# Ring slots, half slots of rounded weights and six feature buffers at other addresses in a three-block transformer kernel

## The reference

```
x = first_block(x, ...)    # h @ w_in; latent attention + a two-way RWKV scan; two branch products; w_out
x = second_block(x, ...)   # x @ w_in_2; conv, pooling and Fourier branches; w_out_2; gated FFN 2048 -> 5632 -> 2048
x = third_block(x, ...)    # c @ w_ada; h @ w_in_3; two attentions; w_out_3; gated FFN 2048 -> 5504 -> 2048
...
def conv_ffn(h, w_up, conv_w, conv_b, w_down):
    u = h @ w_up
    ...
    return (jax.nn.silu(gate) * val) @ w_down
```

## Time and profile before

| | |
|---|---|
| time, median of 3 runs | 3411.87 us (3408.52 to 3414.73) |
| the profiled execution, first to last instruction (span) | 3388.4 us |
| the median's distance from that span | 23.5 us |
| PE busy | 3255.3 us, 96% |
| PEld busy | 3103.4 us, 92% |
| DVE busy | 2275.4 us, 67% |
| ACT busy | 1517.0 us, 45% |
| mean HBM traffic | 196 GB/s |

### The profile page before, as it was taken

How to read it: one execution, slowest core, us unless ns; L and a number is a source line. 1 busy time by engine, 2 the same in 40 slices (tenths; PEclk the granted TensorE clock), 3 DMA queues, 4 the chain that set the end, 5 groups by cost and what they waited for, 6 DMA issues and landing times.

```text
span 3388.4 us, 71888 instructions
## 1 busy us (share of the span) xinstructions
PE 3255.3 (96%) x30322; PEld 3103.4 (92%) x30322; DVE 2275.4 (67%) x2978; ACT 1517.0 (45%) x1835; POOL 74.3 (2%) x154
## 2 busy tenths in 40 slices
PE   8999899999998999999999999999989999999998
PEld 8998888888898769999999999989879899999998
DVE  8776856565687977777655544565656777777545
ACT  5442454443244035544444343453454555545443
POOL 0000100000000000000000000000000000000000
PEclk9999999999999999999999999999999999999999
DMA  8758723232786544677655555534424455555554
GB/s 322 261 204 329 273 86 107 86 108 92 279 346 238 187 161 175 252 290 283 240 190 194 193 195 198 187 127 165 159 100 163 162 191 192 186 187 193 190 197 152
DMA packets 94146, 664.19 MB, mean 196 GB/s; under 512 B 10353, under 2 KB 10993, under 8 KB 15346
## 3 DMA queue, kind: packets, MB, share of 16 engines
q1 hardware_dynamic: 74736, 540.05, 44.4%
q0 software_dynamic: 14400, 104.86, 8.0%
q10 hardware_dynamic: 4802, 16.12, 1.2%
HBM read 654.70 MB, written 6.29 MB: 195 GB/s over the span
## 4 chain that ended last, share of the span: by engine, by line
PE 86%; DVE 9%; ACT 2%; issue 1%; DMA 1%; ACTq 0%; SPq 0%; DVEq 0%
PE ps L463 22%; PE ps L462 22%; PE ps L464 21%; PE ps L434 4%; PE ps L657 4%; PE ps L641 2%; PE ps L493 2%; PE ps L642 2%; PE ps L643 2%; DVE ring_parts L1837 2%; DVE work L1860 1%; DVE work L2113 1%; PE ps L506 1%; DVE ring_parts L1845 1%; PE ps L650 1%
## 5 line engine op out<-in xcount | busy, mean ns | idle before, releaser
L1837 DVE TENSOR_TENSOR ring_parts<-ring,ring_hi 128x1024 fp32r<-128x1024 f32 x866 | 1042.1, 1223 | 701.2 <-ACT ring_hi L1158 687.3
L1158 ACT ACTIVATE ring_hi<-ring 128x1024 fp32r<-128x1024 f32 x866 | 909.4, 1059 | 1141.6 <-PE ps L464 1094.9
L463 PE MATMUL ps<-h_lo,ring_hi 128*128 128x256 f32 x2624 | 729.2, 278 | 0.0
L462 PE MATMUL ps<-h_hi,ring_hi 128*128 128x256 f32 x2112 | 593.1, 281 | 15.8 <-DVE h_lo L1867 8.5
L464 PE MATMUL ps<-h_hi,ring_parts 128*128 128x256 f32 x2112 | 585.1, 277 | 0.0
L463 PEld LDWEIGHTS ps<-h_lo,ring_hi 128*128 128x128 f32 x2624 | 497.7, 190 | 1.4 <-issue 1.2
L462 PE MATMUL ps<-x_hi,ring_hi 128*128 128x256 f32 x1664 | 466.3, 280 | 9.7 <-DVE x_lo L1867 5.8
L463 PE MATMUL ps<-x_lo,ring_hi 128*128 128x256 f32 x1664 | 462.9, 278 | 0.0
L464 PE MATMUL ps<-x_hi,ring_parts 128*128 128x256 f32 x1664 | 461.0, 277 | 0.0
L462 PEld LDWEIGHTS ps<-h_hi,ring_hi 128*128 128x128 f32 x2112 | 397.0, 188 | 18.2 <-issue 9.8
L464 PEld LDWEIGHTS ps<-h_hi,ring_parts 128*128 128x128 f32 x2112 | 397.0, 188 | 0.0
(11 more groups left out here) (471 smaller groups left out, 5781.3 us busy)
## 6 DMA issues: line engine op xcount, KB each, us to landing
ring<-in_weights SPq DMA_DIRECT2D x511, 1024.0 KB, 4.8
work<-in_ada POOLq DMA_DIRECT2D x96, 1024.0 KB, 6.7
work<-in_c_row POOLq DMA_DIRECT2D x4, 1024.0 KB, 5.6
gate_store<-gate_out ACTq DMA_DIRECT2D x8, 512.0 KB, 6.2
work<-gate_store ACTq DMA_DIRECT2D x2, 2048.0 KB, 19.4
resid<-in_lora ACTq DMA_DIRECT2D x9, 256.0 KB, 5.4
resid<-in_x SPq DMA_DIRECT2D x4, 512.0 KB, 6.0
resid<-in_x ACTq DMA_DIRECT2D x1, 2048.0 KB, 28.0
```

The lines of the kernel that those rows point to most:

```text
L462: mm(o, w_hi[:, k, cols], hi(kc), start=(kc == 0 and m % 2 == 0), stop=False, skip_group_check=True)
L463: mm(o, w_hi[:, k, cols], lo(kc), start=False, stop=False, skip_group_check=True)
L1158: A(high_ring(n)[:, 2 * (e % 2) + half, :], ring[:, n % RING, half * (SLOT // 2):(half + 1) * (SLOT // 2)], ACT.Copy)\
L1837: tt(lo, x, high_ring(n)[:, e % 4, :].bitcast(F32), ALU.subtract).then_inc(S("lo_ready"), 1)
```

## The change

Only addresses change. An unused tensor (`ahead`) of 128 bytes puts the ring at place 256, and its slots get 64 bytes between them, so that ring place n % 4 lies at place 256, 320, 384 or 448. The four halves of `ring_hi` get the same gaps and lie at 192, 256, 320 and 384. `ring_hi1` and `ring_hi2` stay as they are. Six feature buffers of the split products move: `m1_hi` to place 64, `hid_lo` to 32, `x_hi` to 64, `x_lo` to 96, `hid3_lo` to 128, `h3_hi` to 192. Some fp32 buffers behind them (`gu`, `p_hi`, `p_lo`, `up3`, `uc`, `mod4`) move along by 128 to 256 bytes. The work area grows by 256 bytes.

```diff
-WORK = 39600
+WORK = 39664
+STAGGER = 16
...
+    ahead = (256 - -(-nc.sbuf_base // 32) * 32) % 512 // 4
+    if ahead:
+        sb("ahead", [P, ahead])
     ring_at = -(-nc.sbuf_base // 32) * 32
-    ring = sb("ring", [P, RING, SLOT])
-    ring_parts = nc.alloc_sbuf_tensor_at("ring_parts", [P, RING, SLOT], F32R, offset=ring_at)
+    assert ring_at % 512 == 256
+    ring = sb("ring", [P, RING, SLOT + STAGGER])[:, :, 0:SLOT]
+    ring_parts = nc.alloc_sbuf_tensor_at("ring_parts", [P, RING, SLOT + STAGGER], F32R, offset=ring_at)[:, :, 0:SLOT]
...
-    M1_HI, M1_LO = own("m1_hi", 14336, DC, T), own("m1_lo", 0, DC, T)
+    M1_HI, M1_LO = own("m1_hi", 14352, DC, T), own("m1_lo", 0, DC, T)
...
-    HID_HI, HID_LO = own("hid_hi", 0, 44, T), own("hid_lo", 11264, 44, T)
-    X_HI, X_LO = own("x_hi", 22528, DC, T), own("x_lo", 26624, DC, T)
+    HID_HI, HID_LO = own("hid_hi", 0, 44, T), own("hid_lo", 11272, 44, T)
+    X_HI, X_LO = own("x_hi", 22544, DC, T), own("x_lo", 26648, DC, T)
...
-    HI = own("ring_hi", 35504, 4, SLOT // 2)
+    HI = own("ring_hi", 35504, 4, SLOT // 2 + STAGGER)[:, :, 0:SLOT // 2]
...
-    HID3_HI, HID3_LO = own("hid3_hi", 4096, FF3_CHUNKS, T), own("hid3_lo", 15360, FF3_CHUNKS, T)
-    H3_HI, H3_LO = own("h3_hi", 26624, DC, T), own("h3_lo", 0, DC, T)
+    HID3_HI, HID3_LO = own("hid3_hi", 4096, FF3_CHUNKS, T), own("hid3_lo", 15392, FF3_CHUNKS, T)
+    H3_HI, H3_LO = own("h3_hi", 26672, DC, T), own("h3_lo", 0, DC, T)
```

More of the change, by code:

```diff
@@ L293, in build_program @@
     ZR_HI, ZR_LO = own("zr_hi", 26624, 8, T), own("zr_lo", 12288, 8, T)
-    M1_HI, M1_LO = own("m1_hi", 14336, DC, T), own("m1_lo", 0, DC, T)
+    M1_HI, M1_LO = own("m1_hi", 14352, DC, T), own("m1_lo", 0, DC, T)
     SHB = w(31296, 2, 4, T)
-    MOD4 = w(34816, FFN2_COLUMNS)
+    MOD4 = w(34848, FFN2_COLUMNS)
     NKK = X[:, 0:8, :]
@@ L338, in build_program @@
     MIX_HI, MIX_LO = own("mix_hi", 22528, DC, T), own("mix_lo", 4352, DC, T)
-    HID_HI, HID_LO = own("hid_hi", 0, 44, T), own("hid_lo", 11264, 44, T)
-    X_HI, X_LO = own("x_hi", 22528, DC, T), own("x_lo", 26624, DC, T)
-    GU, GU2, GU3 = w(30720, 4, T), w(31744, 4, T), own("gu", 32768, 4, T, dt=F32)
-    P2, P2_HI, P2_LO = w(33792, 2, T), own("p_hi", 34304, 2, T), own("p_lo", 33792, 2, T)
+    HID_HI, HID_LO = own("hid_hi", 0, 44, T), own("hid_lo", 11272, 44, T)
+    X_HI, X_LO = own("x_hi", 22544, DC, T), own("x_lo", 26648, DC, T)
+    GU, GU2, GU3 = w(30752, 4, T), w(31776, 4, T), own("gu", 32800, 4, T, dt=F32)
+    P2, P2_HI, P2_LO = w(33824, 2, T), own("p_hi", 34336, 2, T), own("p_lo", 33824, 2, T)
     BROW = w(20736, 2 * COLS)
-    HI = own("ring_hi", 35504, 4, SLOT // 2)
+    HI = own("ring_hi", 35504, 4, SLOT // 2 + STAGGER)[:, :, 0:SLOT // 2]
     Q_SB, K_SB, V_SB = w(4096, 8, T), w(6144, 8, T), w(8192, 2, WIDTH)
@@ L362, in build_program @@
     HS_HI = own("hs_hi", 21568, DC, T)
-    HID3_HI, HID3_LO = own("hid3_hi", 4096, FF3_CHUNKS, T), own("hid3_lo", 15360, FF3_CHUNKS, T)
-    H3_HI, H3_LO = own("h3_hi", 26624, DC, T), own("h3_lo", 0, DC, T)
-    UP3 = w(30720, 8, T + 2)
-    UC = own("uc", 32784, 8, T, dt=F32)
+    HID3_HI, HID3_LO = own("hid3_hi", 4096, FF3_CHUNKS, T), own("hid3_lo", 15392, FF3_CHUNKS, T)
+    H3_HI, H3_LO = own("h3_hi", 26672, DC, T), own("h3_lo", 0, DC, T)
+    UP3 = w(30784, 8, T + 2)
+    UC = own("uc", 32848, 8, T, dt=F32)
     GSIG = UP3[:, 0:4, 2:T + 2]
```

## The result

The changed kernel takes 3438.06 us, median of 3 runs (3436.62 to 3441.16), against 3411.87: 1.0086 times the time before, 95% interval 1.006 to 1.0113. It is slower, where a gain of about 30 us was forecast.

The account below looks back on a forecast made before the run. PE's pace in the split products was taken to bound the kernel. Span 3388.4 less 32 us is 3356.4; with 23.5 us between span and median, 3380 us. Range 3335 to 3440 us.

Parts of the forecast that it names:

- What bounds the kernel: Whole kernel: PE's split-product multiplications, in threes, set about 71% of the end; DVE and ACT have room.
- The reading in steps: Split products: three multiplications take 320 ns plus 6.67 ns steps, one per 64-byte piece; four nearly everywhere, sometimes five.
- What a step is worth: Split products: 6.67 ns more or less on each of 7,600 threes changes the kernel's time by 46 us.
- the factor 0.91: Share of the split products' gain or loss taken to reach the end: 2,406 us in the chain, 2,635 of PE.
- Four places for each of the two weight operands break that up. ... 0.7 step: Split products: spreading the loaded weights avoids collisions with the stream, 0.7 step a three, 32 us less.
- Where the stream lies ... took none away: Third block's output product: features at 256 and 128 only moved stalls within a three, still 346.7 ns.
- The 17th piece: Second block's feed-forward: features moved by 32 and 96 bytes touch 17 pieces, not 16; possibly 15 us lost.
- VectorE, ScalarE, loads at nothing: Subtractions on DVE at most 7 us slower, hidden by waiting; ring loads 0.3 us; nothing added to the range.
- The 23.5 us between span and median: Added to the forecast span of 3356.4 us to give the forecast median, 3380 us.
- Four places are worse than one: Rival, chance 0.28: changing places each half slot brings patterns of five steps or more; 0.6 step, +28 us, 3440 us.
- 4.05 steps: Average steps a three above which the slower rival was said to decide, half slots with one step more outnumbering.
- The places change nothing: Rival, chance 0.22: the steps don't follow from addresses, so the time stays 3412 us, give or take 6.

## Why the prediction was wrong

**What bounds the kernel**: right. PE's pace in the split products set the end; no wait came or went, DVE and ACT waited longer, nothing else moved.

**The reading in steps**: right as a unit. The steady patterns found are 340.0, 346.7, 353.3 and (in some half slots of the changed kernel) 360.0 ns, which with 320 taken off is three, four, five and six times 6.67. Five steps are a pattern of their own where each three takes 353 or 354 ns, as in the earlier trace rows and with the ring at 192 or 448. But the same mean comes from the cycle of four at ring place 256, and other cycles have the means 354.7 and 356.7, which are no whole steps.

**What a step is worth**, 46 us: right, and a little low. The trace after has 1.04 steps more a three, which by the prediction's conversion is 48 us, and the span grew by 51.5. The trace holds 7,488 threes where 7,600 were taken; the factor 0.91 is what is low, for the threes alone grew by 49.2 us, and all of it reached the end.

**"Four places for each of the two weight operands break that up. ... 0.7 step"**: this is the step that failed, with its sign. It rested on the picture of a collision at one relation, which other places would miss. What the runs show in its place is a repeating pattern in which stream and loads stand to each other, and the kernel before happened to sit in a good one. Of the other sets of places tried, only the ring moved by 256 bytes kept it, in the traced execution in the second block alone, and two (ring at 320 or 64) had a better pattern in one block and a worse one in the next. The rest lost it in whole or in part: the ring at one other place no less than at four (1.0106 and 1.0068), the high halves, the features. The whole change without gaps is as slow as with them, so spreading isn't what costs; leaving the pattern costs, about one step in most stretches, from 0.3 (348.7 ns) to 1.8 (358.6). Nothing fell below three steps: no traced kernel has stretches under 339.9 ns a three. So of the four steps one at most was seen to go; spreading the ring did take it away at one of its four places (340 ns), and two of the others paid for it (353 ns).

**"Where the stream lies ... took none away"**: wrong as a ground. It was one pair of places, 256 and 128, against 0 and 0. The features alone raise three of the four stretches by 6.5 to 9.9 ns.

**The 17th piece**: fell. Places of whole 64 bytes cost as much (358.6 ns) as 32 and 96 do (356.6).

**VectorE, ScalarE, loads at nothing**: right. L1842 took 1162 to 1229 ns, its idle time is 737.9 us.

**The 23.5 us between span and median**: wrong as a constant. The changed kernel's traced execution took 3441.16 us with a span of 3439.9, so only 1.3 us lie outside. Before's trace was simply one of the faster executions; unchanged, the kernel took 3388.32 to 3427.61 us in the executions beside the experiments. The forecast didn't fail by this: 3388.4 and 23.5 are the median before, and the gain was taken off that. What it does show is that three executions of before weren't enough to judge a change of 0.9% by: against the sets measured later the change costs 0.9 to 1.2%.

**The rivals.** "Four places are worse than one" came true, with half its mechanism: patterns do settle and the one before was a good one. That its time was nearly met (3440 us; measured 3438.06) is in part luck. Its 4.05 steps as the point from which it decides don't fit the 7 us that the prediction itself asks for, which are 0.15 step. It had 0.6 step, 28 us, on a median before that was high; measured are 1.04 steps, and 51.5 us between the two traces. Its price, though, doesn't come from the changes at half slots, since one place without gaps costs as much, and the point against it, that a boundary doesn't change a pattern, held only for equal places: with four places the pace changes from slot to slot, as the ring alone shows. I gave it 0.28 because it had the evidence of a worse pattern in the trace while nothing in the trace showed a better one than four steps; weighed by that alone it should have been ahead of the gain.

"The places change nothing" fell. Its first ground, the same sum at two places of the stream, was one pair only; its second, several patterns at one set of addresses, was right, and the experiments saw it again. The rule of the Trainium skill beside it ("SBUF — State Buffer", section "Who interferes with whom"), by which TensorE has two independent read ports and never waits on anyone, doesn't agree with this case: its traces show 340 to 360 ns for the same three multiplications at the same clock with no semaphore waited for, according to where their operands lie. That it is the ports at which they wait isn't shown.

**What stays open.** What the pattern is physically: that stream and loads meet in memory fits the runs, but only the dependence on places was shown. What chooses the pattern when PE starts after a wait: at ring place 320 and 64 the 340 ns were held in the second block and not in the third, with the same places. No traced execution held it everywhere. If it could be held, the conversion above gives 46 us less than before; the best seen is 3392.62 us, inside the spread of the kernel before, so no version here beats it. Why the first three executions of the kernel before were at 3408 to 3415 us wasn't traced.

## What to carry to other kernels

When a dense loop of matrix multiplications runs above its column count without any wait, its pace may be a locked pattern that depends on all operand addresses together; a tuned kernel may sit in a good one, and a change of addresses for no other reason than to spread them can lose it: of the fifteen edits tried here one kept the time of before, one is not clear of it (1.003), and none was faster. Measure single places first (here the ring's start repeated after 256 bytes, so four runs 64 bytes apart covered it), and count multiplications in gap-free stretches of the trace, which tells less than 1 ns in a three (one multiplication more in 2600 is 0.1 ns), before trusting a few runs' medians. Any edit that moves buffers, whatever it is for, can carry such a 1% with it; compare it against an edit that moves them alone.

## What the runs showed of the hardware

With a weight load of 128 x 128 for each multiplication of 256 fp32r columns, the granted clock at 1.00 and no wait, a multiplication took 113.3 ns at best in these traces (340.0 a three), never the 106.7 ns that one column a cycle would give; at clock 0.50 it took 213 ns, with nothing on top. The addition depends on the places of the streamed features and of both loaded parts (346.7 ns a three became up to 356.6 when the stream alone moved, 353.8 with the high parts, 353.4 with the ring), and repeats when the remainder's place moves by 256 bytes. It doesn't depend on whether DVE or ACT is at work (346.7 ns with and without). The unchanged kernel ran the same stage at 346.7 ns in one execution and 353.3 in another, and its time spread over 1.2% (3388.32 to 3427.61 us). With the ring at 320 or 64 one execution held 340 ns in the second block and 356.7 in the third, and the times fell into two clusters 1% apart.
